# Feed-forward stages in two phases, with 512-column matmuls over both halves of the input

## The reference, cut to what matters

```
# first block, four times (two layers, two each): D_FF = 2816
a, b = split(rmsnorm(x, g) @ w_in, 2)      # w_in 1024 x 5632
x = x + 0.5 * ((silu(a) * b) @ w_out)      # w_out 2816 x 1024

# second block, twice (once a layer): D_FF_2 = 4096
u = x * (1 + sc2) + sh2
h = square(relu(u @ w_up)) @ w_down        # 1024 x 4096, 4096 x 1024
x = layer_norm(DN_ALPHA * x + (1 + gt2) * h, g, b)
```

## Time and profile before

| | us |
|---|---|
| time, median of 3 runs | 2106.26 (2106.0 to 2118.86) |
| span of the profiled execution | 2110.7 |
| PE busy | 1946.6 |
| DVE busy | 1394.3 |
| ACT busy | 919.1 |
| POOL busy | 764.3 |

### The profile page before, as it was taken

One profiled execution on the slowest core, in us unless ns is written; L12 is line 12 of the kernel. 1 busy time (PEld: TensorE's weight loads), 2 busy tenths in 40 slices (PEclk: granted clock), 3 DMA queues, 4 the chain that ended last, 5 costly groups with the idle time before them and its releaser, 6 DMA issues.

```text
span 2110.7 us, 34770 instructions
## 1 busy us (share of the span) xinstructions
PE 1946.6 (92%) x14460; PEld 1844.3 (87%) x14460; DVE 1394.3 (66%) x1393; ACT 919.1 (44%) x1168; POOL 764.3 (36%) x392
## 2 busy tenths in 40 slices
PE   7999999799989999999799987898999896989998
PEld 7999895699989999857799986788999886889997
DVE  6877544676767776554777759956555589666554
ACT  5444453344434434343333342564444444745443
POOL 3967000346657674020566739700000079000000
PEclk9999896899989998967899988899999998999998
DMA  7877341368676765511477733333655332344551
GB/s 235 270 238 244 98 145 55 100 215 265 227 220 200 256 223 178 179 41 56 154 249 238 243 100 100 111 113 117 188 179 191 120 126 94 121 140 151 180 188 41
DMA packets 288106, 347.61 MB, mean 165 GB/s; under 512 B 15060, under 2 KB 263688, under 8 KB 288008
## 3 DMA queue, kind: packets, MB, share of 16 engines
q1 hardware_dynamic: 287976, 346.18, 50.7%
q10 hardware_dynamic: 32, 0.02, 0.0%
HBM read 345.11 MB, written 1.07 MB: 164 GB/s over the span
## 4 chain that ended last, share of the span: by engine, by line
PE 77%; DVE 16%; ACT 4%; issue 1%; SPq 1%; DMA 1%; ACTq 0%; DVEq 0%
PE bank L765 22%; PE bank L766 22%; PE bank L767 22%; DVE arena L1927 4%; DVE wl L1597 4%; ACT wh L1244 2%; PE bank L940 2%; PE bank L963 2%; DVE xl L1608 1%; DVE xn L1628 1%; PE bank L951 1%; PE bank L1201 1%; PE bank L802 1%; DVE hl L1658 1%; DMA raw<-in_ffn_w_in 1%
## 5 line engine op out<-in xcount | busy, mean ns | idle before, releaser
L1597 DVE TENSOR_TENSOR wl<-raw,wh 128x2048 fp32r<-128x2048 f32 x275 | 736.1, 2682 | 384.3 <-ACT wh L1244 384.2
L765 PE MATMUL bank<-xh,wh 128*128 128x256 f32 x3056 | 889.0, 291 | 70.7 <-DVE xl L1608 33.5
L766 PE MATMUL bank<-xl,wh 128*128 128x256 f32 x3056 | 880.3, 288 | 0.0
L767 PE MATMUL bank<-xh,wl 128*128 128x256 f32 x3056 | 879.7, 288 | 0.0
L1244 ACT ACTIVATE wh<-raw 128x2048 fp32r<-128x2048 f32 x275 | 524.8, 1909 | 403.6 <-PE bank L767 388.0
L765 PEld LDWEIGHTS bank<-xh,wh 128*128 128x128 f32 x3056 | 603.1, 197 | 88.1 <-issue 54.5
L766 PEld LDWEIGHTS bank<-xl,wh 128*128 128x128 f32 x3056 | 603.3, 197 | 0.4 <-issue 0.2
L767 PEld LDWEIGHTS bank<-xh,wl 128*128 128x128 f32 x3056 | 602.7, 197 | 0.0
L707 POOL TENSOR_TENSOR arena<-arena,csil 128x2048 f32<-128x2048 f32 x48 | 185.3, 3859 | 505.3 <-DMA arena<-in_w_ada 486.2
L765 PE MATMUL bank<-hh,wh 128*128 128x256 f32 x1216 | 348.7, 287 | 16.7 <-DVE hl L1658 16.7
L766 PE MATMUL bank<-hl,wh 128*128 128x256 f32 x1216 | 348.0, 286 | 0.0
(11 more groups left out here) (253 smaller groups left out, 1714.2 us busy)
## 6 DMA issues: line engine op xcount, KB each, us to landing
raw<-in_ffn_w_in SPq DMA_DIRECT2D x88, 1024.0 KB, 5.8
arena<-in_w_ada SPq DMA_DIRECT2D x48, 1024.0 KB, 7.5
raw<-in_ffn_w_out SPq DMA_DIRECT2D x44, 1024.0 KB, 5.0
raw<-in_w_in SPq DMA_DIRECT2D x36, 1024.0 KB, 5.0
raw<-in_w_up SPq DMA_DIRECT2D x32, 1024.0 KB, 5.7
raw<-in_w_down SPq DMA_DIRECT2D x32, 1024.0 KB, 4.9
raw<-in_even_w_in SPq DMA_DIRECT2D x12, 1024.0 KB, 5.3
raw<-in_w_out SPq DMA_DIRECT2D x8, 1024.0 KB, 5.1
```

The lines of the kernel that those rows point to most:

```text
L765: pe.matmul(o, wa, ma, start=start, stop=False, **kw)
L766: pe.matmul(o, wa, mb, start=False, stop=False, **kw)
L767: return pe.matmul(o, wb, ma, start=False, stop=stop, **kw)
L1597: dve.tensor_tensor(wl[:, c % RING, :], raw[:, c % RING, :], wh[:, c % RING, :].bitcast(F32), ALU.subtract).then_inc(lo_made.sem, 1)
```

## The change

Every feed-forward stage is split in two phases. In the first all steps of the up product run (22 chunks of w_in in an ffn stage, 16 of w_up in sq), and the activations of all steps stay in `hx`, 128 x (tiles x 2 x 256), high and low part side by side. In the second phase the down product goes through the output in four groups of two tiles of 128 features, each in three (ffn: 8, 8 and 6 k-tiles) or four (sq: 8 each) chunks, so an ffn stage has 34 chunks for the same weights. The input halves lie side by side too (`xx`), and `pair()` replaces `three()` in these stages: W_low meets the high half in 256 columns, W_high meets both halves in one matmul of 512 columns. The bank's left half then holds the two terms with x_high, the right half W_high·x_low, and the two halves have to be added: ScalarE copies the right half out of PSUM and VectorE adds the left one, for a and for b (they lie in banks of their own, 4 and 5, 6 and 7). In the down phase VectorE adds left and right half to x in two operations a tile. Squares and the sums of squares of finished tiles are made inside the down phase, after the second chunk of the next group. The other stages keep `three()`.

Beside that: the rotation's tables and the loads of w_ada, w_uk and the rope inputs move in the queues, `odd` turns w_uk after its first two chunks and not before, a memset of `hpad` moves into the mixer, and the loops unroll three steps and not two.

```diff
-    CHUNKS_OF = {"ffn": 3 * FF_STEPS, "sq": 2 * FF2_STEPS, "even": 16, "odd": 11, "mix": 26}
+    CHUNKS_OF = {"ffn": 2 * FF_STEPS + 4 * len(DOWN["ffn"]), "sq": FF2_STEPS + 4 * len(DOWN["sq"]), "even": 16, "odd": 11, "mix": 26}
...
+DOWN = {"ffn": (8, 8, 6), "sq": (8, 8, 8, 8)}
...
 # TensorE
+            def pair(o, k, hi_w, lo_w, halves, start, stop):
+
+                pe.matmul(o[:, 0:T], lo_w, halves[:, 0, :], start=start, stop=False, skip_group_check=True)
+                return pe.matmul(o.rearrange("p (h t) -> p h t", h=2), hi_w, halves, start=False, stop=stop, skip_group_check=True)
...
                 if st > 0:
-                    pe.wait_ge(h_made.sem, shifted(h_made.at(s, 2 * st), turn, 2 * body))
+                    pe.wait_ge(a_made.sem, shifted(a_made.at(s, st), turn, STEP_BODY))
+                up(c, st, turn, 4)
+                if st > 0:
+                    pe.wait_ge(b_made.sem, shifted(b_made.at(s, st), turn, STEP_BODY))
...
+                up(c + 1, st, turn, 6)
...
+            for g, j, c, k0, n in down_chunks(s):
+                pe.wait_ge(lo_made.sem, c + 1)
+                if g == 0:
+                    pe.wait_ge(hl_made.sem, hl_made.at(s, min(4 * (j + 1), steps)))
+                if g >= 2 and j == 0:
+                    pe.wait_ge(x_ready.sem, x_ready.at(s, 2 * (g - 1)))
+                for m in range(2):
+                    for k in range(n):
+                        last = pair(bank[2 * (g % 2) + m], k0 + k, *tile_of(c, k, m, T), hx[:, k0 + k, :, :],
+                                    start=(k0 + k == 0), stop=(j == len(DOWN[KIND[s]]) - 1 and k == n - 1))
+                last.then_inc(chunk_used.sem, 1)
+                if g >= 1 and j == 1:
+                    pe_stats(NEXT[s], range(2 * g - 2, 2 * g))
...
 # ScalarE, a step of ffn
+                act.activation(ra, psum[:, 4:6, T:2 * T], ACT.Copy).then_inc(right_out.sem, 1)
                 hi(c + RING, turn, per)
+                act.wait_ge(a_made.sem, shifted(a_made.at(s, st + 1), turn, STEP_BODY))
+                act.activation(fs, ra, ACT.Silu).then_inc(act_made.sem, 1)
+                act.wait_ge(chunk_used.sem, shifted(c + 2, turn, per))
+                act.activation(rb, psum[:, 6:8, T:2 * T], ACT.Copy).then_inc(right_out.sem, 1)
+                hi(c + 1 + RING, turn, per)
+                act.wait_ge(h_made.sem, shifted(h_made.at(s, st + 1), turn, STEP_BODY))
+                act.activation(hx[:, mine, 0, :], fh, ACT.Copy).then_inc(hh_made.sem, 1)
...
 # VectorE, a step of ffn
+                dve.tensor_tensor(ra, psum[:, 4:6, 0:T], ra, ALU.add).then_inc(a_made.sem, 1)
                 lo(c + RING, turn, per)
+                dve.tensor_tensor(rb, psum[:, 6:8, 0:T], rb, ALU.add).then_inc(b_made.sem, 1)
+                dve.tensor_tensor(fh, fs, rb, ALU.mult).then_inc(h_made.sem, 1)
+                lo(c + 1 + RING, turn, per)
+                dve.tensor_tensor(hx[:, mine, 1, :], fh, hx[:, mine, 0, :].bitcast(F32), ALU.subtract).then_inc(hl_made.sem, 1)
...
 # VectorE, end of a group of an ffn stage, for both tiles m
+                            dve.scalar_tensor_tensor(out=x[:, k, :], in0=bank[2 * (g % 2) + m][:, 0:T], scalar=0.5, in1=x[:, k, :],
+                                                     op0=ALU.mult, op1=ALU.add).then_inc(left_added.sem, 1)
...
+                        dve.scalar_tensor_tensor(out=x[:, k, :], in0=bank[2 * (g % 2) + m][:, T:2 * T], scalar=scale, in1=x[:, k, :],
+                                                 op0=ALU.mult, op1=ALU.add).then_inc(x_ready.sem, 1)
...
 # SyncE's queue
+                if st in (2, 3):
+                    load_ada(i, st % 2, shifted(ada_summed.at(s, st - 1), turn, 2)) if turn is None else \
+                        load_ada(turn * 2 + st, st % 2, shifted(ada_summed.at(s, st - 1), turn, 2))
+                if st in (8, 10):
+                    n = 6 + (st - 8) // 2
+                    load_ada(n, n % 2, ada_summed.at(s, n - 1))
...
+            for g, j, c, k, n in down_chunks(s):
+                load(c, w_out[:, k:k + n, g * 256:(g + 1) * 256], ("p (k n) -> p k n", {"k": n}))
+                if s in ADA_OF and j == 1:
+                    load_ada(8 + g, g % 2, ada_summed.at(s, 8 + g - 1))
             if s == "ffn3":
+                sp.wait_ge(hl_made.sem, hl_made.at(s))
+                sp.wait_ge(ada_summed.sem, ada_summed.at(s))
...
-    ODD = ["wuk", 0, "small", 1, "index", 2, "csq", "top", 3, "cnorm", "top", 4, "top", "K", 5, "top", "V", "mask", 6]
+    ODD = [0, "small", 1, "wuk", "index", 2, "csq", "top", 3, "cnorm", "top", 4, "top", "K", 5, "top", "V", "mask", 6]
```

More of the change, by code:

```diff
@@ L369, in build @@
             steps = FF_STEPS if kind == "ffn" else FF2_STEPS
-            acc_made.plan(s, 3)
+            right_out.plan(s, steps * (2 if kind == "ffn" else 1))
             if kind == "ffn":
[L372 to L375, removed]
+                b_made.plan(s, steps)
+                act_made.plan(s, steps)
+            for g in (a_made, h_made, hh_made, hl_made):
+                g.plan(s, steps)
+            left_added.plan(s, KT)
+            x_ready.plan(s, KT)
             xstage = s
@@ L538, in sp_ffn @@
             w_out = w_out.rearrange("(k p) n -> p k n", p=P)
[L540 to L546, removed]
             def load_ada(n, slot, times):
@@ L554, in load_ada, with step @@
                              columns(A["w_ada_2"][l], (first + n) * T)).then_inc(ada_loaded[slot].sem, 16)
-            def with_ada(i, st, turn):
-                step(i, st, turn)
+            def step(i, st, turn):
+                c = c0 + n_in * st
+                for half in range(n_in):
+                    load(c + half, columns(w_in, i * 256 + half * FF), A_VIEW, turn, n_in * STEP_BODY)
                 if s == "ffn0" and st == 0:
                     sp_small()
-                if s in ADA_OF and st >= 2:
-                    load_ada(i, st % 2, shifted(ada_summed.at(s, st - 1), turn, body))
-                if s in ADA_OF and st == 1:
+                if s not in ADA_OF:
+                    return
+                if st == 1:
                     if s != "ffn0":
@@ L574, in sp_ffn @@
                     sp.dma_start(dst, src).then_inc(rope_loaded.sem, 16)
-            load(c0 + (n_in + 1) * steps - 1, w_out[:, 2 * steps - 2:2 * steps, :], B_VIEW)
         def sp_even(s):
@@ L803, in pe_rms, with pe_stats @@
-            last.then_inc(stat_made.sem, 1)
+            pe_stats(s, range(6 if KIND.get(x_of[s]) == "ffn" else 0, KT))
+        def pe_stats(s, tiles):
+            for k in tiles:
+                if KIND[s] == "rms":
+                    pe.wait_ge(sq_made.sem, sq_made.at(s, k + 1))
+                else:
+                    pe.wait_ge(x_ready.sem, xr(s, k))
+                src = xn if KIND[s] == "rms" else x
+                last = pe.matmul(bank[STAT][:, 0:T], ones[:, :], src[:, k, :], start=(k == 0), stop=(k == KT - 1))
+            if tiles[-1] == KT - 1:
+                last.then_inc(stat_made.sem, 1)
@@ L1194, in pe_ln @@
         def pe_ln(s):
-            for k in range(KT):
-                pe.wait_ge(x_ready.sem, xr(s, k))
-                last = pe.matmul(bank[6][:, 0:T], ones[:, :], x[:, k, :], start=(k == 0), stop=(k == KT - 1))
-            last.then_inc(stat_made.sem, 1)
+            pe_stats(s, range(6 if s[3] == "b" else 0, KT))
             for k in range(KT):
```

309 lines of the change are left out of this document (149 added, 160 removed).

## The result

The changed kernel takes 2143.82 us (median of 4 runs, 2136.24 to 2147.96), the kernel before on the same chip 2107.94 (2106.0 to 2118.86): a ratio of 1.015, 95% interval [1.0127, 1.0174] (the two medians alone give 1.017). It is 1.5% slower, where I had forecast 3.4% faster and a range that ended at 2098. The profiled execution has a span of 2141.2 us against 2110.7.

What follows compares the result with a forecast made beforehand. TensorE's work per weight tile was taken to bound the kernel, its gaps second. Terms -73-25-5+20+12 = -71 took 2110.7 to 2040 profiled, 2035 us as median (chance 0.58); 8-in-10 range 2008 to 2098.

Steps and rivals of the forecast that it cites:

- pairs in place of triples: Feed-forward weight tiles: two weight loads replace three, 336 ns a tile against 360 at full clock, -73 us.
- stall before the last chunk: Four ffn stages: the 16.7 us wait before the last w_out chunk goes, with slow matmuls behind it, -25 us.
- up steps: Up product of ffn stages: alternating banks for a and b end TensorE's 4.5 us wait for the product, -5 us.
- VectorE against GpSimd: First phase of ffn stages: the two exclude each other while GpSimd sums w_ada, 5 us a stage, +20 (0 to +116).
- sums of squares: Six feed-forward stages: 5.5 us against 3.5, from sums inside the down phase and a tail behind it, +12 us.
- costed at nothing: Down chunk loads, SyncE's wait before the rope inputs, w_ada and w_uk queue moves, memset and others: 0 us.
- rival B: The 13 ns belong to each matmul whatever its length: wide one 226 ns, tile 346, total 2065 us; chance 0.12.
- rival C: The 13 ns belong to the columns: wide matmul 0.24 us, tile stays at 360 ns, total 2096 us; chance 0.15.
- first way to fail: Feed-forward stages: the prediction fails first if the wide 512-column matmul costs more than 226 ns.
- D: First ffn phase: all GpSimd's 66 us hit VectorE, the phase lasts 147 us not 118, total 2131 us; chance 0.08.
- The down chunks: Down phase loads: 1 KB rows land in 5.8 us at the median with 10.8 us to do so; cost nothing.
- the rope: After ffn3: GpSimd's last angle comes about 12 us behind the end, within 3 us of now; cost nothing.

Runs made afterwards that it cites:

- e1: Changed kernel with ScalarE making a finished group's two squares ahead of its `hi` of the chunk three on, not behind it: 2099.74 us, ratio 0.9929 to the kernel before.
- e2: Changed kernel with 641 unused words ahead of `ptmp`, putting it back at its old arena offset: 2130.42 us, ratio 1.0094 to the kernel before.
- e5: Changed kernel with both repairs, squares ahead of ScalarE's `hi` and 641 unused words ahead of `ptmp`: 2088.14 us, ratio 0.9876 to the kernel before.
- e12: e5's kernel with most of GpSimd's sums of w_ada left out, so its result is wrong: 2046.48 us, ratio 0.9703 to the kernel before.
- e16: The kernel before with the same sums of w_ada left out as in e12, so its result is wrong: 2061.51 us, ratio 0.9756.

## Why the prediction was wrong

By the spans, in us:

| step | forecast | measured |
|---|---|---|
| pairs in place of triples | -73 | -29 (1408 tiles by 12.4 ns, 1728 by 6.7) |
| stall before the last chunk, up steps, VectorE against GpSimd | -25 -5 +20 = -10 | -9 (GpSimd costs 41.4 after and 50.6 before) |
| sums of squares | +12 | +42.5 (2141.2 less e1's 2098.7), and the 10.7 of waits that e1 still has and the kernel before has not |
| costed at nothing: what lies behind ptmp | 0 | +12.5 (e2) |
| costed at nothing: even and odd | 0 | +4 (344.3 us before and 348.1 in e5, from the last product matmul of ffn0 and ffn2 to that of even and odd) |
| sum | -71 | +30.5; the rows above give +32 |

Each span is one execution, and the four runs of the changed kernel lie 12 us apart, so a row is good to a few us and the close sum is in part luck. The second row is the weakest: e5 and e12 ran in different jobs, and by the ratios to the kernel before (0.9876 less 0.9703, and 1 less 0.9756 for e16) GpSimd costs 37 and 52 us, and the row would be -15. The gain in the first row is at most 29, since at half clock I count none.

*The step that failed is "Sums of squares".* I priced TensorE's own 16 instructions and the short tail behind the stage, and placed the squares where their data is ready. I didn't write down ScalarE's order there: for each operation that moves into a stream, what is queued ahead of it and what that waits for. I did so for the copies and the silu, and for VectorE's add. For the squares it would have read: behind a `hi` that waits for the chunk TensorE has just finished, with TensorE waiting for the squares. That is a wait of a full `hi` by the code alone, and 12 times a `hi` of 1.9 us is 23 us before anything else (28.4 were measured). The clock is part of the price: e1 has 24.2 us less of these waits and 38 us less at half clock (327.7 us of its span, where the changed kernel has 365.4), which by my estimate is 19 us of delay. Together that is about the 42.5 us of span.

*The second is the size of "Pairs in place of triples".* The mechanism, one load less, gave less than half: -29 us for -73, a miss as large as that of the squares. I took 216 ns for the wide matmul from L802, which is float32 and has 256 columns; the wide fp32r one takes 230 to 236, which is between rival B (226) and rival C (240) and is what the prediction named as its first way to fail. Of the 13 ns beside each matmul, which I gave to the weight load's 107 ns, half are gone when the same three matmuls read from another place (340 ns for three is 113 each, 6.7 over the 106.7 of streaming), so that half belongs to neither of my explanations. Rows at one level in every stage looked like a constant of the instruction, and were a constant of this kernel's memory layout. Neither miss alone would have left the range: 44 us here and 41 for the squares (42.5 + 10.7 - 12) each bring the 2035 to under 2080. A slip of reading beside it: in the six windows of the earlier trace rows TensorE is busy for 97% of the time, not 98.

The Trainium skill, "TensorE: Matmul & The Clock Gate", section "Back-to-back issue gap", puts N/2.4 + 2.5 ns on a warm matmul, by which a pair would take an estimated 325 ns. It calls this the gap of a single matmul in isolation, which the prediction left out, and says that in a stream of weight loads and matmuls both set the spacing. No run here has under 340 ns for a triple or 347 for a pair, so the formula alone doesn't give the time of these streams. The Trainium skill's step-by-step section on the same page says that loading the next weights doesn't steal read bandwidth from the running matmul. No run here tests that: the pitch depends on where the moving operand lies, by up to 20 ns in 360, but whether the weight loads have a part in it stays open.

*VectorE's lock* was the rival that I feared (D), with +116 at most. The joint term came out as forecast, -9 against -10, but by luck in its parts: the waits for VectorE in the new first phase are 8.6 us, 2 a stage where I had put 5, and VectorE is busy for 85 to 93% of a stage's first 40 us, not over 95; the stall that I booked as a gain from the new order is a cost of GpSimd too. In e12 GpSimd's work is worth 41 us to the repaired kernel, most of it by the lock; D's mechanism is there, and as large before.

*What I costed at nothing.* The down chunks and the rope did cost nothing visible. SyncE's queue costs nothing visible in the changed kernel either (ScalarE waits 4.82 us for mix0's weights there, beside the stops for the squares), but 6 to 7 us once the squares are repaired, as e1's last stop shows: the wait ahead of mix0's weights, which the prediction saw and priced at nothing. The move of the arena's tensors I hadn't costed at all: I had followed which instructions moved, not which addresses. The turn of w_ada behind ffn2 is slower (9.69 us for 48 loads, L1169, in place of 6.54), and the granted clock over it is 0.53 in place of 0.81. In e1, without the stops inside the phase, the four turns take 7.3 to 8.6 us, so the stops are part of the reason; the rest is not shown.

```profile
845.16 9.69 PE L1169 MATMUL bank<-ones,arena 128*128 128x1 f32 x48
```

## What to carry to other kernels

When work moves into another engine's stream, write down that stream's order around it and look for the loop: does anything ahead of it wait for the step that waits for it? Where a duration looks constant, ask whether the rows behind it also share a layout; before pairing instructions to save 13 ns each, shift one operand by 64 or 192 bytes and look at the pitch. And price a lock by leaving out the other engine's work in both kernels, since a stall of before may already be its price.

## What the runs showed of the hardware

- The pitch of 256-column fp32r matmuls depends on where the moving operand lies: with the weights left in place, an offset of 0, 256 or 512 bytes gives 360 ns for three, 128 gives 356 (360 in the last stage), 64 and 192 give 353 or 340. With the same addresses the level still changes between phases.
- A 512-column fp32r matmul takes 0.230 or 0.236 us at full clock and a pair 347 or 353 ns. That is 7 to 13 ns less than three of 256 columns at the bad place, and the right place alone gives the triples 7 to 20.
- The time of a GpSimd addition of 128x512 with one operand shifted by 641 words is 1153 against 1354 ns.
- The fastest kernels measured that do the whole computation are the one before with 192 bytes of padding (2067.66 us) and the changed one with both repairs, triples and 192 bytes (2068.46). The second has triples in the new order; pairs with 192 bytes were not run. The repairs and the padding together bring the new order no further than the padding alone brings the old one.
